# Weights laid out chunk by chunk on the host, and six modulation chunks of the second layer summed on VectorE

## The reference

```python
def adaln(cvec, w, b):
    m = jax.nn.silu(cvec) @ w + b              # w: 1024 x 6144, six vectors of 1024
    return [m[..., None, i, :] for i in range(6)]
for l in range(DEPTH):                          # DEPTH = 2
    sh1, sc1, ga1, sh2, sc2, ga2 = adaln(c, w_mod[l], b_mod[l])
    csh1, csc1, cga1, csh2, csc2, cga2 = adaln(c_ctx, w_mod[l], b_mod[l])
    cols_c = split_columns(modulate(rms_norm(ctx, g_norm1[l]), csh1, csc1) @ w_in[l])
    cols_x = split_columns(modulate(rms_norm(x, g_norm1[l]), sh1, sc1) @ w_in[l])
    y_gla_c, s_f, s_b = gla_branch(cols_c, *gla_p, s0, s0)        # chunked linear attention
    y_gla_x, _, _ = gla_branch(cols_x, *gla_p, s_f, s_b)
    y_loc_x = local_branches(cols_x, *loc_p, axial_dwconv, row_mean)
    x = x + ga1 * (jnp.concatenate([y_gla_x, y_loc_x], axis=-1) @ w_out[l])
    ...                                         # ctx likewise, in layer 0 only
    m_x = modulate(rms_norm(x, g_norm2[l]), sh2, sc2)
    x = x + ga2 * hier_moe(m_x, *moe_p)         # 32 experts, two per token
```

## Time and profile before

| | |
|---|---|
| time, median of 3 (lowest to highest) | 1389.33 us (1388.03 to 1390.4) |
| the profiled execution: its span, first to last instruction | 1386.3 us |
| PE busy | 1177.8 us (85%), 12667 instructions |
| DVE busy | 591.4 us (43%) |
| ACT busy | 202.4 us (15%) |
| POOL busy | 216.6 us (16%) |
| moved by DMA | 485.55 MB in 106192 packets, mean 350 GB/s |
| DMA queue of SP (q1) | 97696 packets, 471.62 MB, 85.0% of 16 engines' span |
| mean granted clock of PE | 0.951 |

### The profile page before, as it was taken

One profiled execution on the slowest core, in us unless ns is written; L12 is line 12 of the kernel. 1 busy time (PEld: TensorE's weight loads), 2 busy tenths in 40 slices (PEclk: granted clock), 3 DMA queues, 4 the chain that ended last, 5 costly groups with the idle time before them and its releaser, 6 DMA issues.

```text
span 1386.3 us, 31515 instructions
## 1 busy us (share of the span) xinstructions
PE 1177.8 (85%) x12667; PEld 646.8 (47%) x12668; DVE 591.4 (43%) x1350; ACT 202.4 (15%) x431; POOL 216.6 (16%) x387
## 2 busy tenths in 40 slices
PE   6999999989999997899996799997887666887665
PEld 3446454455555554455453685554443333443332
DVE  2391154357777765676765551544111010111002
ACT  3103311340000000000000324132000000000001
POOL 3105011011111111111111320102111010111000
PEclk9999999999999999999999999998998887999887
DMA  9921584799999999999999675879999999999995
GB/s 336 321 94 62 212 304 130 277 391 374 415 420 421 418 417 421 420 417 418 421 419 413 222 271 187 314 306 357 419 419 416 417 422 419 418 418 422 417 419 227
DMA packets 106192, 485.55 MB, mean 350 GB/s; under 512 B 8986, under 2 KB 27810, under 8 KB 90016
## 3 DMA queue, kind: packets, MB, share of 16 engines
q1 hardware_dynamic: 97696, 471.62, 85.0%
q0 software_dynamic: 6416, 9.42, 2.0%
q10 hardware_dynamic: 2032, 3.84, 0.8%
HBM read 485.92 MB, written 4.23 MB: 354 GB/s over the span
## 4 chain that ended last, share of the span: by engine, by line
PE 61%; SPq 13%; DMA 10%; DVE 6%; issue 5%; ACT 4%; DVEq 0%; POOL 0%; ACTq 0%; POOLq 0%
PE bank L1805 14%; SPq L892 12%; PE bank L1830 8%; PE bank L1501 7%; PE bank L1820 6%; PE bank L1682 6%; DMA ring<-in_expert_w_out 5%; DMA work<-in_expert_w_out 5%; PE bank L1602 4%; PE bank L1394 3%; DVE resid L1933 2%; ACT msb L1124 2%; PE bank L1811 2%; PE bank L1518 2%; PE bank L1568 1%
## 5 line engine op out<-in xcount | busy, mean ns | idle before, releaser
L1805 PE MATMUL bank<-ring,msb 128*32 128x256 f32 x3456 | 224.9, 404 | 67.6 <-DMA ring<-in_expert_w_in 47.2
L1933 DVE TENSOR_TENSOR resid<-bank,resid 128x512 f32<-128x512 f32 x376 | 233.1, 682 | 95.2 <-PE bank L1830 95.2
L1124 ACT ACTIVATE msb<-bank 128x256 f32<-128x256 f32 (+2 forms) x190 | 69.0, 364 | 868.2 <-PE bank L1805 769.7
L1805 PEld LDWEIGHTS bank<-ring,msb 128*32 128x32 f32 x3456 | 109.4, 114 | 171.3 <-issue 61.6
L2219 DVE COPY msb<-bank 128x256 f32<-128x256 f32 x85 | 35.6, 419 | 261.9 <-PE bank L1771 261.7
L1081 POOL COPY work<-work 128x256 f32<-128x256 f32 x86 | 34.2, 398 | 656.2 <-issue 335.6
L1820 PE MATMUL bank<-ring,msb 128*32 128x256 f32 x1728 | 110.5, 398 | 29.2 <-DMA ring<-in_expert_w_out 20.3
L1830 PE MATMUL bank<-work 32*128 32x256 f32 x1376 | 105.9, 425 | 5.1 <-DVE msb L2242 4.6
L1071 POOL DMA_INDIRECT work<-h_rows,gidx x86 | 88.8, 1033 | 76.6 <-POOL gidx L1068 67.4
L1501 PE MATMUL bank<-actT,ring 128*128 128x256 f32 (+1 forms) x320 | 97.2, 466 | 0.5 <-ACT actT L1180 0.5
L1830 PEld LDWEIGHTS bank<-work 32*128 32x128 f32 x1376 | 66.4, 198 | 48.7 <-issue 32.5
(11 more groups left out here) (292 smaller groups left out, 1148.4 us busy)
## 6 DMA issues: line engine op xcount, KB each, us to landing
ring<-in_expert_w_in SPq DMA_DIRECT2D x80, 2048.0 KB, 25.2
ring<-in_expert_w_out SPq DMA_DIRECT2D x40, 2048.0 KB, 28.2
ring<-in_w_mod SPq DMA_DIRECT2D x24, 2048.0 KB, 12.2
states<-in_expert_w_in SPq DMA_DIRECT2D x21, 2048.0 KB, 27.1
work<-in_expert_w_out SPq DMA_DIRECT2D x21, 2048.0 KB, 28.1
actT<-in_expert_w_in SPq DMA_DIRECT2D x20, 2048.0 KB, 23.3
ring<-in_w_in SPq DMA_DIRECT2D x7, 2048.0 KB, 12.6
ring<-in_w_out SPq DMA_DIRECT2D x4, 2048.0 KB, 8.2
```

The source lines that it names most:

```text
L1124: return act.activation(o, i, func, **kw)
L1805: ins = mm(PS[1][q, 0:256], xeT[:, c % 2, BLK * (c // 2):BLK * (c // 2 + 1)], w[k][:, 256 * g:256 * (g + 1)], start=c == 0, stop=c == KT - 1)
L1933: ins = tt(v, PS[4 + g].rearrange("p (t n) -> p t n", t=2), v, ALU.add)
```

## The change

Host layout (`in_chunks`): `w_mod`, `w_in`, `w_out` and `expert_w_out` are rearranged on the host so that each chunk which the kernel loads lies in one piece, 16 KB in a row for each partition (9 KB for the `w_in` chunk of 288 columns). Before, a load of `expert_w_out` or `w_out` had four runs of 4 KB per partition, one of `w_in` or `w_mod` eight of 2 KB (the small `w_in` chunk 1.1 KB, the first four chunks of `w_mod` 1 KB). `expert_w_in` had 16 KB in a row before and is unchanged.

Six chunks by rows (`by_rows`): chunks 4 to 9 of layer 1 are also turned on the host, so that channels of the output lie on the partitions: partition p holds for four output channels all 1024 weights. DVE multiplies each of these four pieces by silu(c), which stands in every partition in `msb`, and sums (`sum_by_rows`, four `tensor_tensor_reduce` over 128x1024 each). PE's products and transposes, ACT's copies and DVE's reductions of these chunks go. ACT loads `c` into every partition early in layer 1 and applies silu. SP waits for DVE (`s_byrow`) before it refills their slots, and the slots of the stream of layer 1 are dealt out anew.

```diff
+def by_rows(l, n):
+    return l == DEPTH - 1 and 4 <= n < 10
...
+def in_chunks(name, a):
+    if name == "w_mod":
...
+        rest = a[:, :, 2 * D:].reshape(DEPTH, P, KT, 8, 512).transpose(0, 3, 1, 2, 4)
+        turned = a[:, :, 2 * D:].reshape(DEPTH, D, 4, P, 2, 4).transpose(0, 2, 4, 3, 5, 1).reshape(DEPTH, 8, P, -1)
...
+    if name == "expert_w_out":
+        return a.reshape(DEPTH, NE, 4, P, D).transpose(0, 1, 3, 2, 4).reshape(DEPTH, NE, P, 4 * D)
+    return a
...
-    slots += ([1, 2, 3, 1, 2, 1, 2] if l == 0 else [1, 2, 1, 3, 2, 1, 3])
-    return slots + ([1, 0, 2] + [0, 2, 0, 2] if l + 1 < DEPTH else [1, 0, 3])
+    slots += ([1, 2, 3, 1, 2, 1, 2] if l == 0 else [1, 2, 1, 2, 3, 1, 2])
+    return slots + ([1, 0, 2] + [0, 2, 0, 2] if l + 1 < DEPTH else [0, 1, 2])
...
-        ewout = t_in["expert_w_out"].rearrange("l e (k p) n -> (l e) p k n", k=4)
+        ewout = t_in["expert_w_out"].rearrange("l e p (k n) -> (l e) p k n", k=4)
...
-                        sp.wait_ge(made, jobs.at[last_use(stream(l)[before])] + 1)
+                        held_by = stream(l)[before]
+                        if held_by[1] == "mod" and by_rows(*held_by[::2]):
+                            sp.wait_ge(s_byrow, held_by[2] - 3)
+                        else:
+                            sp.wait_ge(made, jobs.at[last_use(held_by)] + 1)
...
+                    act.dma_start(msb[:, :], t_in["c"][0].rearrange("(o d) -> o d", o=1).broadcast_to([P, D])).then_inc(s_crow, 16)
...
+                if l == DEPTH - 1:
+                    act.wait_ge(s_crow, 16)
+                    copy(msb[:, :], msb[:, :], ACT.Silu).then_inc(s_silrow, 1)
...
+            def sum_by_rows(l, n):
+                s, v = chunks.where[(l, "mod", n)]
+                dve.wait_ge(slot_ready[s], v)
+                if n == 4:
+                    dve.wait_ge(s_silrow, 1)
+                for j in range(4):
+                    part = slot[s][:, D * j:D * (j + 1)]
+                    at = 4 * (n % 2) + j
+                    ins = dve.tensor_tensor_reduce(part, part, msb[:, :], 1.0, 0.0, ALU.mult, ALU.add,
+                                                   mt[:, 0, at:at + 1])
+                ins.then_inc(s_byrow, 1)
...
+                if rows:
+                    dve.wait_ge(s_mpar[l], 16 * 2)
+                    sum_by_rows(l, 4)
+                    sum_by_rows(l, 5)
+                    shift_scale(l, 2)
                 dve.wait_ge(s_lab, l + 1)
...
+                if rows:
+                    sum_by_rows(l, 6)
                 got(dve, "A", l, "var")
...
```

More of the change, by code:

```diff
@@ L60 @@
 POOL_N = POOL_X + CTX + 2 * PADW
+def by_rows(l, n):
+    return l == DEPTH - 1 and 4 <= n < 10
+def in_chunks(name, a):
+    if name == "w_mod":
+        first = a[:, :, 0:2 * D].reshape(DEPTH, P, KT, 2, 4, 256).transpose(0, 4, 1, 2, 3, 5)
+        rest = a[:, :, 2 * D:].reshape(DEPTH, P, KT, 8, 512).transpose(0, 3, 1, 2, 4)
+        turned = a[:, :, 2 * D:].reshape(DEPTH, D, 4, P, 2, 4).transpose(0, 2, 4, 3, 5, 1).reshape(DEPTH, 8, P, -1)
+        rest = rest.reshape(DEPTH, 8, P, -1)
+        rest = np.stack([np.where(np.array([by_rows(l, n) for n in range(4, 12)])[:, None, None], turned[l], rest[l])
+                         for l in range(DEPTH)])
+        return np.concatenate([first.reshape(DEPTH, 4, P, -1), rest], axis=1)
+    if name == "w_in":
+        rows = a.reshape(DEPTH, KT, P, N_IN).transpose(0, 2, 1, 3)
+        return np.concatenate([rows[:, :, :, u:v].reshape(DEPTH, -1) for u, v in WIN], axis=1)
+    if name == "w_out":
+        return a.reshape(DEPTH, 2, 4, P, D)[:, ::-1].transpose(0, 1, 3, 2, 4).reshape(DEPTH, 2, P, 4 * D)
+    if name == "expert_w_out":
+        return a.reshape(DEPTH, NE, 4, P, D).transpose(0, 1, 3, 2, 4).reshape(DEPTH, NE, P, 4 * D)
+    return a
 def layer_tiles(l):
@@ L594, in norm_base, with win @@
             return sum(TILES + LAYER_T[i] for i in range(l)) + TILES * n
[L596 to L599, removed]
+        wmod = t_in["w_mod"]
+        wout = t_in["w_out"]
+        def win(l, n):
+            a, b = [P * KT * sum(v - u for u, v in WIN[0:i]) for i in (n, n + 1)]
+            return t_in["w_in"][l, a:b].rearrange("(p k n) -> p k n", p=P, k=KT)
         ewin = t_in["expert_w_in"].rearrange("l e (p h k) n -> (l e) h p (k n)", h=2, k=4)
-        ewout = t_in["expert_w_out"].rearrange("l e (k p) n -> (l e) p k n", k=4)
+        ewout = t_in["expert_w_out"].rearrange("l e p (k n) -> (l e) p k n", k=4)
         def slot_view(key):
@@ L1276, in _ @@
                     done(copy(qkvg[:, t, a:512], bank[:, a:512]), "A", l, "qkv", t)
-                    if t in (1, 3):
+                    if t in (1, 3) and not by_rows(l, 2 * t + 4 - t // 3 * 2):
                         mod_rows(l, 2 * t + 4 - t // 3 * 2)
@@ L1951, in quarter @@
                 dve.wait_ge(s_quarter, 4 * l + q + 1)
-            def shift_scale(l, i):
-                for h in range(2):
-                    bank = take(dve, l, "modT", i, h)
-                    rows = bank[:, :].rearrange("p (k g c) -> p c k g", k=4, g=4)[:, 0:2, :, :]
-                    done(dve.tensor_reduce(mt[:, :, 4 * h:4 * h + 4], rows, AX_X, ALU.add), "D", l, "modT", i, h)
-                got(dve, "D", l, "modT", i, 1)
+            def sum_by_rows(l, n):
[9 more added lines that the diff above has]
+                ins.then_inc(s_byrow, 1)
+            def shift_scale(l, i):
+                if by_rows(l, 2 * i):
+                    dve.wait_ge(s_byrow, 2 * i - 2)
+                else:
+                    for h in range(2):
+                        bank = take(dve, l, "modT", i, h)
+                        rows = bank[:, :].rearrange("p (k g c) -> p c k g", k=4, g=4)[:, 0:2, :, :]
+                        done(dve.tensor_reduce(mt[:, :, 4 * h:4 * h + 4], rows, AX_X, ALU.add), "D", l, "modT", i, h)
+                    got(dve, "D", l, "modT", i, 1)
                 b = bc(bmod[:, i, :], 1, 2)
@@ L2117, in _ @@
                 dve.wait_ge(s_un, l + 1)
-                dve.wait_ge(s_mpar[l], 16 * 2)
-                shift_scale(l, 2)
+                if rows:
+                    sum_by_rows(l, 7)
+                else:
+                    dve.wait_ge(s_mpar[l], 16 * 2)
+                    shift_scale(l, 2)
                 for m in range(2):
@@ L2134, in _ @@
                     tt(ex[:, 3 * d + 2, :, :], k, ex[:, 3 * d + 2, :, :], ALU.mult).then_inc(s_qd, 1)
-                shift_scale(l, 4)
+                if not rows:
+                    shift_scale(l, 4)
                 heads = const("heads")
```

60 lines of the change are left out of this document (37 added, 23 removed).

## The result

The changed kernel takes 1380.53 us (median of 4 runs, 1377.31 to 1383.43) beside 1389.42 us of the kernel before: a ratio of 0.9938, with a 95% interval of 0.9915 to 0.996. Run again later it took 1381.47 us (6 runs, 1379.61 to 1382.81), a ratio of 0.9949 (0.9936 to 0.9961). It is faster by 7 to 9 us, not by the 12.6 that I forecast: the time lies in the wide range, 1370 to 1386, and above the forecast's own, 1372 to 1379.

What follows compares the result with a forecast made beforehand. DMA transfers after a lull were taken to bound the expert stages, PE the mixtures. Span 1386.3 - 16.8 (layout) + 4.3 (late entry) = 1373.8, plus 3.0 to the median: 1376.8 us; own range 1372 to 1379, 8 in 10 1370 to 1386.

Steps and rivals of the forecast that it cites:

- (a): Rival: PE paces stage 0 up to 540 us, so only 4.2 of 8.7 us count there: 1381.3 us, chance 0.14.
- (b): Rival: DVE's sums run at half rate, 2.4 us each, and hold up the queries: 1389.2 us, no change, chance 0.12.
- Part 1: Layout in both expert stages: longer rows save 0.3 us on each of 56 chunks after the lulls, 16.8 us.
- The cover in stage 0: Stage 0: 4.2 us of queued work at the tightest place keeps the DMA queue from drying, so 8.7 us count in full.
- Part 3: Mixture 1: DVE's 24 sums, 31 us, start `la` 3.2 us late; PE idles, then half clock costs 1.7 us.
- x: Mixture 1: how much earlier PE's chain runs from the queries' transposes on: 5.7 us, bounds 4 to 7.4.
- d: Mixture 1: time of one DVE sum over 128x1024 with its accumulator read, 1.3 us, bounds 1.1 and 2.4.
- 7.4 us without any clock: Mixture 1: PE's gain with the last turn gone, before 1.7 us is taken off for the half clock.
- Part 4: Entry to stage 1: new slots hold expert loads behind the local projection; DMA engines enter 10.0 - x late, 4.3 us.
- The 3.0 us from span to median: Whole kernel: the median of the runs was taken to be 3.0 us above the profiled span, 1373.8 to 1376.8 us.
- (c): Rival: row length makes no difference to the stream, only the late start of the queue remains: 1393.6 us, slower, chance 0.08.
- (d): Rival: slots pace stage 1, so the late start costs nothing and PE's 7.4 us count in full: 1365.1 us, chance 0.06.

Runs made afterwards that it cites:

- `expert_w_out` alone: The kernel before with only `expert_w_out` laid out in one piece, the other weights, products and slots as they were: 1377.2 us, ratio 0.9917.
- The slots of before: The changed kernel with the slots of layer 1's stream dealt as in the kernel before: 1370.21 us, ratio 0.9866.

## Why the prediction was right or wrong

**Stretches, bounds and sign: right.** Transfers after a lull and the late entry set the end; the earlier trace rows were the right views. Faster, at 0.84, came true. That the time lies in the wide range is in part luck: that range was stretched for (a) and (b), neither of which happened. The forecast's own range failed on one side, since it let the layout bring up to 3 us more and nothing less.

**Part 1, 16.8 us: the mechanism right, the size too large.** Measured 5.8 + 6.6 = 12.4 us; 12.0 with `expert_w_out` alone. The step that failed is the price of 0.3 us a chunk, from the duration of single packets; 0.20 to 0.27 were measured. With 4.3 to 4.4 us it is the largest error that both profiles of the changed kernel show. The earlier trace rows held the warning: the shares were 99.8% and 102.3%, so the short packets overlapped a little, and what a packet takes is then more than what it costs. By the GB/s of the same two groups, 2.097 MB / 0.411 and / 0.423, the price is 0.15 us; the truth lies between, as far from the one as from the other. Stage 0 is 5.8 and 6.0 us shorter in the two profiles, and not 8 to 9. The cover in stage 0 held: rival (a) is out, since the window of 322 to 540 us has the full 425 GB/s. The 5 us from the Trainium skill's fixed cost a packet (DMA: Bandwidth & Descriptors, "Why small descriptors are slow") was too small by more than half.

**Part 3, x = 5.7 us: right in direction, too large.** Measured x = 2.1 in the first profile (the transposes L1672 start 8.65 us earlier, L1679 7.9 earlier, the mixture's first dense products 5.8: 775.35 for 781.12) and 4.5 in the second (8.8 less 4.3), inside the bounds of 4 to 7.4. `la` late and PE idle before `var` were as forecast. The delay of `la` was too small in both, the clock's share in the first only.
- `la` was 4.7 us late and not 3.2 (832.76 against 833.83 less 5.8). Chunk 5 took 9.1 us to land and not 8.2: 0.9. Its sums beside POOL: 0.6.
- The sums: I took d = 1.3 us. Alone it is 1.15; beside POOL 1.65 in these steps. Rival (b), half rate, is out. The rule for it in the Trainium skill, Vector Engine (DVE) Microarchitecture Reference, "Points that are easy to get wrong", is given for the scalar-tensor-tensor instruction; the trace names this one `CUSTOM_DVE_ANT_0`, and for it the rule doesn't hold. Yet a rule that I did not weigh does hold: the Trainium skill, SBUF — State Buffer, section "SBUF: two separate sides", has VectorE with two SBUF inputs and GpSimd share one pair of ports by an exclusive lock. The trace agrees that the two hold each other up: a sum of 1.22 us takes 1.65 to 1.74 beside POOL, and a POOL operation of 0.63 to 0.72 us takes 1.42 to 1.59 beside a sum.
- The half clock cost 3.0 us behind the first pause and not 1.7: the drop was 6.8 us long, twice the 3.4 of the earlier trace rows. In the second profile it was short again and cost 1.5.
- In the first profile it came also behind the pause of 2.25 us before the queries, which I had kept for a bound: from the first transpose to L1679 3.44 us, against 2.56 in the second profile, so 0.9. What makes a drop long or short, no run here shows.

From the 7.4 us without any clock, less 1.5, 3.0 and 0.9, that leaves 2.0; in the second profile, less 1.5 and 1.5, 4.4.

**Part 4, 4.3 us late: right in kind, and hung on x.** With x = 2.1 and 4.5 the formula 10.0 - x gives 7.9 and 5.5 us; in bytes the mixture is 8.8 and 6.6 us longer, about 1 us more each time, which stays open. The slots of before alone take 10 to 11 us off. The sum with measured terms, 1386.3 - 12.4 - 1.2 + 8.8, is 1381.5. The 3.0 us from span to median were off as well: each run takes 1.8 to 1.9 more than its span, and the other 1.2 stood there because the profiled execution of the kernel before was a fast one.

**The rivals.** (a) named a time, 1381.3, close to the measured one, by chance: its mechanism is out. (c) is out by the 425 GB/s; the late start without the layout's gain is the changed kernel with the old `expert_w_out`, 6 us slower than before where (c) charged 4.3. (d) is out since the late start cost the 10 to 11 us that the slots of before bring back.

## What to carry to other kernels

Work moved to an idle engine is not free: ask what waits behind it in that engine's order (here `la`, and through it PE), and whether PE's time was won where PE was the last to come. When slots are dealt anew, follow each load ahead to the wait that now frees it; one list of numbers was worth more here than the change. Where the share is above 1, price a transfer both by the duration of its packets and by the GB/s of a pure stretch, and take the two as bounds: 0.3 and 0.15 us a chunk here, 0.22 measured. And profile a kernel twice before a difference of 2 us in one stage is explained.

## What the runs showed of the hardware that I had not expected

- A multiply with an accumulated sum over 128x1024 float32, both operands in SBUF, takes 1.22 us on DVE and starts every 1.15, its accumulator read of 0.08 hidden. Beside a POOL operation on two SBUF operands it takes 1.65 to 1.74, and POOL's 1.42 to 1.59 in place of 0.63 to 0.72. DVE's reciprocal with one operand (1.74 us with POOL beside it, 1.75 without) and POOL's operation beside it (0.72) are not slowed.
- In a queue that never dries, rows of 4 KB for a third of the chunks cost 1.4% of the rate and for two thirds 2.8% (425, 419, 413 GB/s).
- After a pause of PE of 4.93 us the work behind it ran at half clock and took 3.0 us more; with the pause filled it ran at full clock. In a second execution of the same kernel, with the same pause, it took 1.5 us more. The drops do not come in the same place in each run either: in two of the faster kernels one stood behind a pause of 1.23 us at 820 us, and in a third it did not. That may be part of the spread of 1 to 6 us within one kernel; no run here separates it.
